# Two groups of output columns computed together at the start of each projection stage, in a one-core hybrid decoder step

## The reference

```python
x = x + 0.5 * post1(SwiGLU_1(pre1(x)))
x = x + postm(W_out concat[norm_a(DilatedSWA), norm_b(StickBreaking), norm_m(MemCross)])
x = x + 0.5 * post2(SwiGLU_2(pre2(x)))
...
def swiglu(x, w_gu, w_down):
    g, u = jnp.split(x @ w_gu, 2, axis=-1)
    return (jax.nn.silu(g) * u) @ w_down
...
k, v = jnp.split(rms_norm(mem, g_mem) @ w_mem_kv, 2, axis=-1)
```

## Time and profile before

| | us |
|---|---|
| median of 3 runs | 2477.51 (2476.82 to 2481.85) |
| time of the profiled execution | 2474.81 |
| its span from the first to the last instruction | 2472.8 |

### The profile page before, as it was taken

The page is one execution under the profiler, slowest core; times in us unless marked ns, Lnnn a source line. Parts: engine busy times, 40 slices in busy tenths (PEclk is TensorE's granted clock), DMA queues, the critical chain, the costliest instruction groups (busy, mean ns, idle before and its releaser), DMA issues.

```text
span 2472.8 us, 41417 instructions
## 1 busy us (share of the span) xinstructions
PE 2192.2 (89%) x16853; PEld 2085.5 (84%) x16853; DVE 1435.4 (58%) x3208; ACT 914.5 (37%) x1183; POOL 463.7 (19%) x412
## 2 busy tenths in 40 slices
PE   6899999999999969856454997978999999999996
PEld 6899999999999959846442445978999999999996
DVE  6655555555555674578886224556555555555556
ACT  3344344444344443211113143334444344344443
POOL 4510000000000160744442011134000000000004
PEclk9999999999999979977775998989999999999999
DMA  7355555555555527388688994433555555555551
GB/s 253 133 185 181 185 175 186 178 181 172 187 187 171 188 85 242 110 274 264 219 267 289 320 330 143 153 123 134 188 175 179 186 177 180 181 186 181 178 186 54
DMA packets 229120, 467.72 MB, mean 189 GB/s; under 512 B 11873, under 2 KB 12770, under 8 KB 228146
## 3 DMA queue, kind: packets, MB, share of 16 engines
q1 hardware_dynamic: 227426, 460.71, 55.4%
q0 software_dynamic: 1504, 4.36, 0.5%
HBM read 456.34 MB, written 8.68 MB: 188 GB/s over the span
## 4 chain that ended last, share of the span: by engine, by line
PE 74%; DVE 11%; DMA 6%; POOL 3%; issue 3%; SPq 2%; ACT 1%; POOLq 0%; DVEq 0%; ACTq 0%
PE ps L446 23%; PE ps L447 23%; PE ps L448 23%; DVE k_cache L1278 7%; DMA k_cache<-win_k 3%; PE ps L687 1%; DMA v_cache<-win_v 1%; POOL acc L1543 1%; SPq L358 1%; DVE y L1146 1%; DMA k_cache<-sb_k 1%; DVE wl L1084 1%; PE ps L699 1%; SPq L357 1%; DVE xl L1096 1%
## 5 line engine op out<-in xcount | busy, mean ns | idle before, releaser
L446 PE MATMUL ps<-xh,wh 128*128 128x264 f32 (+1 forms) x3840 | 1122.2, 292 | 170.3 <-POOL wl L1605 109.8
L1084 DVE TENSOR_TENSOR wl<-raw,wh 128x1024 fp32r<-128x1024 f32 x605 | 749.9, 1243 | 759.5 <-ACT wh L772 759.4
L772 ACT ACTIVATE wh<-raw 128x1024 fp32r<-128x1024 f32 x656 | 690.5, 1058 | 1221.4 <-PE ps L448 990.9
L447 PE MATMUL ps<-xl,wh 128*128 128x264 f32 (+1 forms) x3840 | 1115.0, 290 | 0.0
L448 PE MATMUL ps<-xh,wl 128*128 128x264 f32 (+1 forms) x3840 | 1113.6, 290 | 0.0
L446 PEld LDWEIGHTS ps<-xh,wh 128*128 128x128 f32 x3840 | 749.1, 195 | 184.1 <-POOL wl L1605 114.3
L447 PEld LDWEIGHTS ps<-xl,wh 128*128 128x128 f32 x3840 | 748.0, 195 | 0.0
L448 PEld LDWEIGHTS ps<-xh,wl 128*128 128x128 f32 x3840 | 745.9, 194 | 0.0
L446 PE MATMUL ps<-hh,wh 128*128 128x264 f32 x1408 | 400.0, 284 | 0.0
L448 PE MATMUL ps<-hh,wl 128*128 128x264 f32 x1408 | 399.9, 284 | 0.0
L447 PE MATMUL ps<-hl,wh 128*128 128x264 f32 x1408 | 399.8, 284 | 0.0
(11 more groups left out here) (207 smaller groups left out, 1045.0 us busy)
## 6 DMA issues: line engine op xcount, KB each, us to landing
raw<-w_gu SPq DMA_DIRECT2D x176, 1024.0 KB, 4.9
raw<-w_down SPq DMA_DIRECT2D x88, 1024.0 KB, 5.0
raw<-w_in SPq DMA_DIRECT2D x40, 1024.0 KB, 6.7
k_cache<-sb_k SPq DMA_DIRECT2D x128, 256.0 KB
v_cache<-sb_v SPq DMA_DIRECT2D x128, 256.0 KB
raw<-w_out SPq DMA_DIRECT2D x16, 1024.0 KB, 5.1
raw<-w_mem_kv SPq DMA_DIRECT2D x8, 1024.0 KB, 10.2
k_cache<-win_k SPq DMA_DIRECT2D x16, 384.0 KB
```

The costliest lines, as they stand in the source:

```text
L446: pe.matmul(out, w_hi, rh(k0 + kk), start=first and kk == 0, stop=False)
L447: pe.matmul(out, w_hi, rl(k0 + kk), start=False, stop=False)
L772: act.activation(wh[:, c % UNIT_SLOTS], raw[:, raw_slot, 2 * (c % 2):2 * (c % 2) + 2], ACT.Copy).then_inc(hi_made, 1)
L1084: dve.tensor_tensor(wl[:, c % UNIT_SLOTS], raw[:, (c // 2) % RAW_SLOTS, part], wh[:, c % UNIT_SLOTS].bitcast(F32), ALU.subtract).then_inc( ...
```

## The change

The first two groups of every stage run together over all eight banks: for each two k rows PE does the unit of the first group, then that of the second. So a pass takes two units, and 16 units need the same 8 passes of x. `lower` and `upper` run two passes ahead of the splits in the list, the updates three. The chunks of these two groups hold two k rows of both groups; the loads take them so (in pieces of 512 columns for the memory and the nets, of 1024 columns for the input and output projection). The sum of squares is put ahead of the last unit, into the unused columns of banks 0 and 1 (bank 4 for the memory), PE no longer waits for the root, and `take_gate` and its like follow after both groups.

```diff
+        def raw_unit(c):
+            chunk, n = divmod(c, 2)
+            beside = CH_IN <= chunk < CH_IN + 8 or CH_OUT <= chunk < CH_OUT + 8
+            return raw[:, chunk % RAW_SLOTS, n:4:2] if beside else raw[:, chunk % RAW_SLOTS, 2 * n:2 * n + 2]
...
+            def load_pair(n, c, weights, cols, first=False):
+                if not first:
+                    sp.wait_ge(lo_made, 2 * n - 6)
+                src = weights.rearrange("(k p) (g n) -> p g k n", p=P, n=512)[:, cols, 2 * c:2 * c + 2]
+                sp.dma_start(raw[:, n % RAW_SLOTS].rearrange("p (g k) n -> p g k n", g=2), src
+                             ).then_inc(w_loaded[n % RAW_SLOTS], 16)
+            def load_neighbours(n, c, weights, col):
+                sp.wait_ge(lo_made, 2 * n - 6)
+                src = weights.rearrange("(k p) n -> p k n", p=P)[:, 2 * c:2 * c + 2, 512 * col:512 * col + 1024]
+                sp.dma_start(raw[:, n % RAW_SLOTS].rearrange("p (k g) n -> p k (g n)", g=2), src
+                             ).then_inc(w_loaded[n % RAW_SLOTS], 16)
...
+            def two_groups(v, width, banks, done, guard, ready, between):
+                for c in range(8):
+                    pe.wait_ge(ready, 2 * c + 2)
+                    for n in range(2):
+                        if c == 7 and n == 1:
+                            between()
+                        unit(v + 2 * c + n, (2 * c + n) % UNIT_SLOTS, lambda k: xh[:, k, 0:width],
+                             lambda k: xl[:, k, 0:width], 2 * c, banks[n], width, c == 0, c == 7, done[n], guard[n])
+            def sum_beside(name):
+                pe.wait_ge(squared[name], KT)
+                pe.matmul(ps[0][:, TOK:512], ones[:], acc[:, 0, 0:512 - TOK], start=True, stop=True,
+                          skip_group_check=True)
+                pe.matmul(ps[1][:, TOK:2 * TOK + TOK - 512], ones[:], acc[:, 0, 512 - TOK:TOK], start=True, stop=True,
+                          skip_group_check=True).then_inc(summed, 1)
...
-                group(u0, TOK, 0, g_done[l], guard_g, xl_ready[name])
                 bank_free()
-                sum_partitions(name, 7)
-                pe.wait_ge(rooted, nth(name))
-                group(u0 + 8, TOK, 4, u_done[l], guard_u)
+                two_groups(u0, TOK, (0, 4), (g_done[l], u_done[l]), (guard_g, guard_u), xl_ready[name],
+                           lambda: sum_beside(name))
...
             (ACT, feed-forward net)
+                for c in range(2):
+                    upper_pair(name, c, ready, ready_n, gain)
                 for c in range(8):
-                    for k in (2 * c, 2 * c + 1):
-                        upper(name, k, ready, ready_n + k + 1, gain)
-                    split(u0 + c + AHEAD)
+                    split(u0 + 2 * c + AHEAD)
+                    upper_pair(name, c + 2, ready, ready_n, gain)
                     if name != "ffn1":
-                        squares_behind(name, c)
-                if name != "ffn1":
-                    squares_behind(name, 8)
-                take_root(name, 7, D_MODEL, before)
+                        squares_behind(name, c + 1)
+                    split(u0 + 2 * c + 1 + AHEAD)
+                root_beside(name, before)
                 silu(0)
-                for c in range(8, 16):
-                    split(u0 + c + AHEAD)
                 upper_h(0, 0)
...
             (DVE, input projection)
             update_pair("mix", 0, G_POST1)
             update_pair("mix", 1, G_POST1)
+            lower_pair("mix", 0, G_PREM)
+            update_pair("mix", 2, G_POST1)
+            lower_pair("mix", 1, G_PREM)
             for c in range(8):
-                update_pair("mix", c + 2, G_POST1)
-                for k in (2 * c, 2 * c + 1):
-                    lower("mix", k, G_PREM)
-                split(u_in + c + AHEAD)
+                split(u_in + 2 * c + AHEAD)
+                update_pair("mix", c + 3, G_POST1)
+                lower_pair("mix", c + 2, G_PREM)
+                split(u_in + 2 * c + 1 + AHEAD)
             invert("mix", r_pre)
             dve.wait_ge(r_ready, nth("mix"))
...
             take_projection(0, 0, qT, 0)
-            for c in range(8, 16):
-                split(u_in + c + AHEAD)
             take_projection(0, 1, qT, 4)
```

More of the change, by code:

```diff
@@ L810, in _, with upper_pair @@
                 split(c)
-            for c in range(8):
-                for k in (2 * c, 2 * c + 1):
-                    upper("mem", k, turn_read, k + 1, G_MEM)
-                split(c + AHEAD)
-            take_root("mem", 0, D_MODEL, None, width=N_MEM)
-            for c in range(8, 16):
-                split(c + AHEAD)
+            def upper_pair(name, c, ready, n, gain):
+                if c < 8:
+                    for k in (2 * c, 2 * c + 1):
+                        upper(name, k, ready, n + k + 1, gain)
+            for c in range(2):
+                upper_pair("mem", c, turn_read, 0, G_MEM)
+            for c in range(8):
+                split(2 * c + AHEAD)
+                upper_pair("mem", c + 2, turn_read, 0, G_MEM)
+                split(2 * c + 1 + AHEAD)
+            act.wait_ge(summed, nth("mem"))
+            act.activation(root[:, 0:N_MEM], ps[4][:, N_MEM:2 * N_MEM], ACT.Sqrt, scale=1.0 / D_MODEL, bias=eps[:, 0:1]
+                           ).then_inc(rooted, 1)
             for i in range(4):
@@ L1120, in _, with lower_pair @@
                 split(c)
+            def lower_pair(name, c, gain):
+                if c < 8:
+                    for k in (2 * c, 2 * c + 1):
+                        lower(name, k, gain)
+            for c in range(2):
+                lower_pair("mem", c, G_MEM)
             for c in range(8):
-                for k in (2 * c, 2 * c + 1):
-                    lower("mem", k, G_MEM)
-                split(c + AHEAD)
+                split(2 * c + AHEAD)
+                lower_pair("mem", c + 2, G_MEM)
+                split(2 * c + 1 + AHEAD)
             invert("mem", r_post, N_MEM)
@@ L1182, in ffn @@
                     bring_in(1)
+                lower_pair(name, 0, gain)
+                if bring_in is not None:
+                    bring_in(2)
+                lower_pair(name, 1, gain)
                 for c in range(8):
+                    split(u0 + 2 * c + AHEAD)
                     if bring_in is not None:
-                        bring_in(c + 2)
-                    for k in (2 * c, 2 * c + 1):
-                        lower(name, k, gain)
-                    split(u0 + c + AHEAD)
+                        bring_in(c + 3)
+                    lower_pair(name, c + 2, gain)
+                    split(u0 + 2 * c + 1 + AHEAD)
                 invert(name, r_pre)
@@ L1486, in _ @@
             normed(1)
+            lower_pair("out", 0, None)
+            normed(2)
+            lower_pair("out", 1, None)
             for c in range(8):
-                normed(c + 2)
-                for k in (2 * c, 2 * c + 1):
-                    lower("out", k, None)
-                split(u_out + c + AHEAD)
+                split(u_out + 2 * c + AHEAD)
+                normed(c + 3)
+                lower_pair("out", c + 2, None)
+                split(u_out + 2 * c + 1 + AHEAD)
             for g in range(4):
-                if g > 0:
+                if g > 1:
                     for c in range(8):
```

106 lines of the change are left out of this document (58 added, 48 removed).

## The result

The changed kernel takes 2432.8 us at the median (four executions, 2427.08 to 2438.22), the kernel before beside it 2477.16 (four, 2471.01 to 2481.85): a ratio of 0.983, 95% interval 0.980 to 0.985. The forecast was 2428, its range 2419 to 2446. The profiled execution took 2427.08 us with a span of 2425.2; that is 47.6 less than the span before, where the sum of the steps was 49.3.

What follows compares the result with a forecast made beforehand. PE was taken to be bound by waits and order, DVE's work too heavy in first groups; stage gains 2.2 + 6.0 + 14.2 + 10.9 + 16.0 = 49.3 us off 2474.8 gave 2425.5, on the median's footing 2428, range 2419 to 2446.

Steps and rivals of the forecast that it cites:

- The memory: Memory stage: 47.7 against 52.75 us, 5.0 less; 2.8 us back for the root now on the path; gain 2.2.
- a stall above some 2 us is paid twice: PE, read from the profile before: such a stall costs idle time and then a slow unit at a lower clock.
- price of 1.8 us for a slow unit: PE's unit after a long stall: 1.8 us more, as 4.73 us was read against 2.91.
- First net: First net's two groups: 50.0 against 55.96 us, with 0.65 us idle before the second step; gain 6.0.
- Input projection and second net: The two heavy stages: 50.5 against 64.73 us, gain 14.2, and 51.5 against 67.52 us, gain 16.0.
- The term of 1.0 us for DVE: Each heavy stage: PE's delay from DVE falling behind, taken as 1.0 us between bounds of 0 and 3.7.
- The cover of 3.8 us: Heavy stages: lead of x and splits covers 3.8 us of DVE's delay, second split ending at 7.8, due at 11.6.
- the upper bound of 3.7 us a stage: Heavy stages: DVE up to 0.94 us behind a pass, 7.5 over eight passes, less 3.8 covered.
- Rival A: DVE and POOL by turns pace the heavy stages, always contended: 2442 us with the cover, 2450 without; chance 0.14.
- Rival B: The first three stages' gain, 22 us, is lost in the attention: 2451 us; chance 0.06.
- Rival C: New loads: 24 two-block chunks landing in 9.8 us make PE wait 4.0 us each, 2524 us in all; chance 0.04.
- The product's chain: Both nets: splits from unit 19 on wait 8.1 us behind it, PE has 9.1; no cost, bound 2 us a net.

Runs made afterwards that it cites:

- Lower_twice: Changed kernel with one more two-input DVE instruction per k row in the input projection and second net, into a buffer nothing reads; median 2443.63 us.
- pair_only: Changed kernel without the lead: groups still paired, x made just in time; median 2495.28 us, ratio 1.008 to the kernel before.
- mix_apart: Changed kernel with the input projection alone as before (its loads, lists and sum); median 2454.91 us, ratio 0.990 to the kernel before.
- Root_first: Changed kernel with the memory's unit 18 splits moved behind the root, reciprocal and reads; median 2425.13 us, ratio 0.979 to the kernel before.
- tail_moved: Changed kernel with unit 18's splits behind root and reads (memory, first net), heavy stages' last squares one pass earlier; 2433.54 us, ratio 0.982 to the kernel before.
- root_gate: Changed kernel with unit 18's splits behind root and reads in memory and first net, squares not moved; 2429.48 us, ratio 0.980 to the kernel before.

## Why the prediction was right, and where it was not

- **What bounds.** That the first group has too much of DVE's work and the second too little, and that order and balance are both needed, is what the two halves show: 2455 by the lead alone, 2495 by the pairs alone, 2433 together.
- **The memory: the step that failed.** "With the reads of the values that follow I take 2.8 us back": the idle was right, 3.05 us measured. But PE then ran the x transposes, and those of the memory's keys and values behind them, at a clock of 0.56, for 5.7 us more. 4.0 us of gain in the window (forecast 5.0) less 9.0 makes the loss of 5.0. The prediction had read that a stall above some 2 us is paid twice and did not apply it to its own stall. Nor would its price of 1.8 us for a slow unit have done: behind this stall stood not one slow unit but 15.6 us of transposes, at 0.50 from 77.10 us to their end.
- **First net.** Window 49.13 against 49.3; the idle ahead of step 2 was 1.11 us and not 0.65, the half microsecond by which the gain fell short.
- **Input projection and second net.** Too small by 1.7 and 2.9 us. The term of 1.0 us for DVE was 0, the sum's wait 0.99 and not 1.35, the unit after it not slower, the sum itself 0.69, the start 1.8 sooner and not 1.5; the second net's first unit took 4.7 us (1623.25 to 1627.95) and not 5.67.
- **The cover of 3.8 us** was the right reason for taking DVE's term near the lower bound. Lower_twice loads a pass to 6.76 us, the price that the prediction gave for the always contended pass (6.75), and PE waits 0.3 us more in the window (1.26 against 0.99). So the upper bound of 3.7 us a stage was too high at that price: it let all eight passes fall behind, and only five hold scaled rows.
- **Rival A** therefore fails at its second half. DVE does pace its own passes (5.88 us, no idle), but the lead takes it. The stretch by POOL is real: a pair of two-input instructions on DVE took 0.89 us where POOL rested (pair_only) and 1.88 beside it. The Trainium skill's page "SBUF — State Buffer", section "Who interferes with whom", has the two engines take a shared port pair by turns; the trace agrees, and the conclusion that this rival is the likelier one did not follow.
- **Rival B.** In the profiles the stretch got 1.3 us shorter up to its sum, and on the mean of the executions it is 588 us before and after: no loss is seen there. Four executions between 583 and 594 us can't exclude a loss of a few microseconds, and the 589 to 597 of the experiments leave it open.
- **Rival C.** The eight chunks of each net that come as two column blocks landed in 4.8 to 5.4 us in the trace, far below the 7.9 from which it decides, the memory's eight in 5.2 to 15.1 us (4.9 to 15.9 before), and PE waits for none of them within the pairs.
- **The product's chain.** No wait for unit 19 on: it cost nothing, as said.
- **The total** came out near by luck, since two errors met: 7.2 us too much in the memory, 4.6 too little in the heavy stages.

## What to carry to other kernels

Work that an engine must do for the first of several groups can be spread over more units by computing groups side by side, but only if it also stands ahead, in the engine's list, of what waits for the consumer: here either half alone gave at most half of the gain, and pairing alone lost time. When a change takes cover from a chain (here the root, which had a whole group beside it), cost the idle of PE and then ask at what clock the work behind it runs: here the fallen clock cost almost twice as much as the idle. And a saved wait is won only if the next thing in the chain is early too, as the moved squares showed.

## What the runs showed that was not expected

- An idle of 3.05 us ahead of the x transposes brought them down to a clock of 0.56, half the speed for nearly all of 15.6 us, not at once but after the first four groups of transposes (0.52 us apart, then 0.82). It came so in all four profiles with such an idle (3.05 to 3.09 us; the three others are lower_twice, mix_apart and pair_only, at 0.52 to 0.56). With 1.05 us of idle, or 0.68, the same transposes ran at 1.00 throughout.
- The prediction's reading "a stall above some 2 us was paid twice" holds for the units it read, but not always. Root_first, tail_moved and root_gate have the same memory stage and the same idle of 2.22 us ahead of the first net; its first unit ran at 1.00 in the first and at 0.64 and 0.65 in the others, and the window of the first net's two groups was 1.5 us shorter for it (47.6 against 49.1). The length of the idle alone does not settle the clock. In this order, 4.70 us from the first net's start:

```profile
85.83:90.53 4.70, 4.70 (x39) 4.70 (x40) 4.70 (x5) 2.98 (x5) 4.54 (x6) 1.00 0.05 7
...
85.29:89.99 4.70, 4.70 (x26) 4.70 (x27) 4.70 (x5) 1.93 (x4) 4.54 (x6) 0.64 0.02 5
...
85.89:90.59 4.70, 4.70 (x26) 4.70 (x27) 4.70 (x5) 2.06 (x5) 4.54 (x6) 0.65 0.05 5
```

- DVE and POOL fell into a rhythm in which DVE's splits always met a resting POOL, so a pass took 5.88 us and neither 4.1 nor 6.75. Without the lead POOL rested through DVE's whole chain (0.89 us a pair): who meets whom is set by the order of the lists, not by the share of busy time.
- The stretch with the attention varies by 4 to 20 us among the executions of one kernel, if the rest of the kernel is taken as fixed: often more than the steps told apart here. Its cause was not found.
